# Expert 0 of a mixture-of-experts stage: gathering its rows in two halves with features on partitions

## The reference

```python
logits = (xt @ w_router + b_router)
top_vals, top_idx = lax.top_k(logits, TOP_K)
top_gates = jax.nn.softmax(top_vals, axis=-1)
...
def expert_block(args):
    xb, e = args
    gate = xb @ w_gate[e] + b_gate[e]
    up = xb @ w_up[e] + b_up[e]
    gate = jnp.minimum(gate, SWIGLU_LIMIT)
    up = jnp.clip(up, -SWIGLU_LIMIT, SWIGLU_LIMIT)
    glu = gate * jax.nn.sigmoid(SWIGLU_ALPHA * gate)
    return (glu * (up + 1.0)) @ w_down[e] + b_down[e]
```

## Time and profile before

| | |
|---|---|
| median of 3 runs | 1621.6 us (1621.21 to 1623.56) |
| span of the profiled execution | 1622.2 us |
| TensorE busy | 97% of the span |
| VectorE, ScalarE, GpSimd busy | 38%, 29%, 18% |
| transfers of phase B | 2,048 KB each |
| expert stage | from about 124.5 us to about 1036 us |

### The profile page before, as it was taken

One profiled execution on the slowest core, in us unless ns is written; L12 is line 12 of the kernel. 1 busy time (PEld: TensorE's weight loads), 2 busy tenths in 40 slices (PEclk: granted clock), 3 DMA queues, 4 the chain that ended last, 5 costly groups with the idle time before them and its releaser, 6 DMA issues. The chain is left out here.

```text
span 1622.2 us, 22330 instructions
## 1 busy us (share of the span) xinstructions
PE 1576.5 (97%) x9026; PEld 914.1 (56%) x9026; DVE 623.6 (38%) x1169; ACT 468.3 (29%) x703; POOL 286.7 (18%) x180
## 2 busy tenths in 40 slices
PE   9999999999999999999999999999999999999998
PEld 8843333333333333233233232598898899999986
DVE  7743212121212112121121121486586444478852
ACT  6421111111111111111111111466555554454443
POOL 3500000000000000000000000274234324445552
PEclk9999999999999999999999999999999999999999
DMA  9698999999999999999999999544324125555542
GB/s 350 216 379 339 427 427 426 426 429 426 427 427 428 427 426 427 427 428 428 428 428 428 427 428 428 216 153 156 105 105 156 58 99 208 179 168 187 182 182 104
DMA packets 93976, 507.66 MB, mean 313 GB/s; under 512 B 9020, under 2 KB 34665, under 8 KB 69321
## 3 DMA queue, kind: packets, MB, share of 16 engines
q1 hardware_dynamic: 93656, 505.97, 77.2%
q10 hardware_dynamic: 240, 0.55, 0.1%
HBM read 505.46 MB, written 1.05 MB: 312 GB/s over the span
## 5 line engine op out<-in xcount | busy, mean ns | idle before, releaser
L190 POOL TENSOR_TENSOR low<-ring,high 128x1024 fp32r<-128x1024 f32 x81 | 201.6, 2491 | 1275.6 <-ACT high L187 1275.5
L1684 PE MATMUL ps<-ring,x 128*64 128x512 f32 x1536 | 341.9, 595 | 21.4 <-DMA ring<-in_w_up 21.4
L1684 PEld LDWEIGHTS ps<-ring,x 128*64 128x64 f32 x1536 | 106.0, 137 | 253.2 <-issue 206.4
L187 ACT CAST high<-ring 128x1024 fp32r<-128x1024 f32 x162 | 167.8, 1049 | 192.7 <-PE ps L1850 115.7
L1846 PE MATMUL ps<-hTh,high 128*128 128x256 f32 x768 | 189.1, 284 | 0.5 <-PEq L2794 0.5
L1847 PE MATMUL ps<-hTl,high 128*128 128x256 f32 x768 | 188.4, 283 | 0.0
L1720 PE MATMUL ps<-ring,x 128*64 128x512 f32 x752 | 170.5, 595 | 0.0
L190 DVE TENSOR_TENSOR low<-ring,high 128x1024 fp32r<-128x1024 f32 x81 | 108.9, 1345 | 129.7 <-ACT high L187 129.6
L1846 PEld LDWEIGHTS ps<-hTh,high 128*128 128x128 f32 x768 | 147.3, 192 | 1.9 <-issue 1.5
L1847 PEld LDWEIGHTS ps<-hTl,high 128*128 128x128 f32 x768 | 147.4, 192 | 0.0
L1544 DVE TENSOR_SCALAR hT<-ps 128x512 f32<-128x512 f32 x32 | 22.1, 691 | 294.5 <-PE ps L1684 294.5
(11 more groups left out here) (503 smaller groups left out, 2105.3 us busy)
## 6 DMA issues: line engine op xcount, KB each, us to landing
ring<-in_w_down SPq DMA_DIRECT2D x52, 2048.0 KB, 32.8
ring<-in_w_gate SPq DMA_DIRECT2D x48, 2048.0 KB, 31.5
ring<-in_w_up SPq DMA_DIRECT2D x48, 2048.0 KB, 31.1
ring<-in_w_in SPq DMA_DIRECT2D x22, 2048.0 KB, 7.8
extra<-in_w_gate SPq DMA_DIRECT2D x16, 2048.0 KB, 32.0
extra<-in_w_up SPq DMA_DIRECT2D x16, 2048.0 KB, 29.8
extra<-in_w_down SPq DMA_DIRECT2D x14, 2048.0 KB, 34.7
ring<-in_w_up SPq DMA_DIRECT2D x22, 1024.0 KB, 7.2
```

Source lines behind the costliest of these rows:

```text
L187: eng.copy(hi, self.raw(u)).then_inc(self.sem("high_split"), 1)
L190: eng.tensor_tensor(lo, self.raw(u), hi.bitcast(F32), ALU.subtract).then_inc(self.sem(who + "_split"), 1)
L1684: last = pe.matmul(bank[h * CAP:(h + 1) * CAP, :], xg[:, c, kh, :], w[:, c, h * 512:(h + 1) * 512], start=False, stop=kh == 1 and c == 3)
```

## The change

The rows of expert 0 are no longer gathered with tokens on partitions. A new function `gather_columns` multiplies blocks of `xn` (128 tokens x 128 features) as weights with the picks (128 tokens x 64 places), so that the result has features on partitions at once. It does one half of the features, four blocks with two matmuls each (one for each half of the tokens). The first half is gathered at the end of phase A into bank 2 (the bank of G_), the second in phase B into bank 1 (ROWS), between the first and the second half of the gate product of expert 0. VectorE multiplies each half with its part of `g2` from its own bank. `rows_kept(0)` on ScalarE and `turned(0)` on TensorE are gone. The gate biases of expert 0 are added between the halves of its gate product, the up biases directly ahead of its up product; the first gate matmul now starts the bank (`start=True`). Experts 1 to 31 are as before.

```diff
-            pe.wait_ge(banks.free[ROWS_BANK], banks.uses[ROWS_BANK])
+            pe.wait_ge(banks.free[TURNED_BANK], banks.uses[TURNED_BANK])
             pe.wait_ge(sem("picks"), NT)
-            gather_rows(pe, banks.ps[:, ROWS_BANK, :], env["pick"], xn).then_inc(banks.full[ROWS_BANK], 1)
+            gather_columns(pe, banks.ps[:, TURNED_BANK, :], env["pick"], xn, 0).then_inc(banks.full[TURNED_BANK], 1)
...
+def gather_columns(pe, bank, pick, xn, h):
+
+    for c in range(4):
+        for t in range(NT):
+            last = pe.matmul(bank[:, c * CAP:(c + 1) * CAP], xn[:, t, h * 512 + c * P:h * 512 + (c + 1) * P], pick[:, t, :],
+                             start=t == 0, stop=t == NT - 1)
+    return last
...
-            v.tensor_scalar(hot[:, 0, :], ones[0:64, 0:CAP], fold[0:64, 0:1], None, ALU.mult).then_inc(sem("hot"), 1)
+            for h, use in enumerate((G_, ROWS)):
+                bank = bank_take(v, use, 0)
+                gains = env["g2"][:, 4 * h:4 * h + 4].unsqueeze(2).to_broadcast([P, 4, CAP])
+                bank_free(v.tensor_tensor(xg[:, :, h, :], bank[:, 0:4 * CAP].rearrange("p (c j) -> p c j", c=4), gains,
+                                          ALU.mult), use)
+                if h == 0:
+                    v.tensor_scalar(hot[:, 0, :], ones[0:64, 0:CAP], fold[0:64, 0:1], None, ALU.mult).then_inc(sem("hot"), 1)
...
-            gathered(0)
...
-            rows_kept(0)
...
-            turned(0)
             pe.wait_ge(sem("btab_in"), 48)
+
+            def second_columns():
+
+                bank_full(gather_columns(pe, bank_claim(pe, ROWS, 0), pick, xn, 1), ROWS)
...
+                whole = rnd is None and r == 0
+                both = [(0, GATE, bank_claim(pe, GATE, i)), (1, UP, None if whole else bank_claim(pe, UP, i))]
...
+                if not whole:
+                    pe.wait_ge(sem("hot"), i + 1)
+                    for m, use, bank in both:
+                        bias(m, bank)
                 bank_moved(pe, G_, i)
                 for m, use, bank in both:
                     for kh in range(2):
+                        if whole and m == 0 and kh == 1:
+                            second_columns()
+                            pe.wait_ge(sem("hot"), i + 1)
+                            bias(0, bank)
+                            bank_moved(pe, ROWS, i)
+                        if whole and m == 1 and kh == 0:
+                            bank = bank_claim(pe, UP, i)
+                            bias(1, bank)
```

More of the change, by code:

```diff
@@ L1366, in _ @@
             keep_busy(pe, banks.ps[:, banks.at["lgt"][0], :], ones, 2)
-            pe.wait_ge(banks.free[ROWS_BANK], banks.uses[ROWS_BANK])
+            pe.wait_ge(banks.free[TURNED_BANK], banks.uses[TURNED_BANK])
             pe.wait_ge(sem("picks"), NT)
-            gather_rows(pe, banks.ps[:, ROWS_BANK, :], env["pick"], xn).then_inc(banks.full[ROWS_BANK], 1)
-ROWS_BANK = 1
+            gather_columns(pe, banks.ps[:, TURNED_BANK, :], env["pick"], xn, 0).then_inc(banks.full[TURNED_BANK], 1)
+ROWS_BANK, TURNED_BANK = 1, 2
+def gather_columns(pe, bank, pick, xn, h):
[4 more added lines that the diff above has]
+    return last
 def gather_rows(pe, bank, pick, xn):
@@ L1671, in expert, with bias @@
                 nxt = i + 1 if rnd is None else pe.snap(i + 1)
-                pe.wait_ge(sem("hot"), i + 1)
-                both = [(0, GATE, bank_claim(pe, GATE, i)), (1, UP, bank_claim(pe, UP, i))]
-                for m, use, bank in both:
+                whole = rnd is None and r == 0
+                both = [(0, GATE, bank_claim(pe, GATE, i)), (1, UP, None if whole else bank_claim(pe, UP, i))]
+                def bias(m, bank):
                     for h in range(2):
                         pe.matmul(bank[h * CAP:(h + 1) * CAP, :], hot[32 * m:32 * m + 32, r % 2, :],
-                                  btab[32 * m:32 * m + 32, h * 512:(h + 1) * 512], start=True, stop=False)
+                                  btab[32 * m:32 * m + 32, h * 512:(h + 1) * 512], start=m == 1 or not whole, stop=False)
+                if not whole:
+                    pe.wait_ge(sem("hot"), i + 1)
+                    for m, use, bank in both:
+                        bias(m, bank)
                 bank_moved(pe, G_, i)
@@ L1684, in expert @@
                                 last = pe.matmul(bank[h * CAP:(h + 1) * CAP, :], xg[:, c, kh, :],
-                                                 w[:, c, h * 512:(h + 1) * 512], start=False,
+                                                 w[:, c, h * 512:(h + 1) * 512], start=whole and m == kh == c == 0,
                                                  stop=kh == 1 and c == 3)
```

## The result

| | median | range | span of the profiled execution |
|---|---|---|---|
| before | 1621.6 us (5 runs) | 1621.21 to 1623.56 | 1622.2 us |
| changed | 1626.18 us (5 runs) | 1623.96 to 1628.83 | 1624.4 us |

The ratio is 1.0027, 95% interval 1.0017 to 1.0038: the change made the kernel slower by 4.6 us. I had forecast 1622.1 us and no measurable change. The median lies above the range. The sum had the right sign, but with +0.5 us a ninth of the size.

What follows compares the result with a forecast made beforehand. The DMA stream of weight pieces bounds the expert stage. Piece 1 -1.6, piece 2 -0.5, piece 5 0 to +0.9; the latest wins, +0.5: span 1622.2 to 1622.7, less 0.6 gives 1622.1 us, range 1620.4 to 1623.6.

Steps and rivals of the forecast that it cites:

- The sum: Expert 0's changes added up: TensorE 1.5 us late from the up product on, +0.5 us at the end.
- the slack: How late expert 0's weight piece 5 may be issued without delaying the stream: 0.6 to 1.5 us.
- The frame: Expert stage: it ends when the last weight piece lands, so an edit counts by its effect on the stream.
- Part 1: Path to expert 0's first gate half product: it starts at 127.8 instead of 129.38, piece 1 issued 1.6 us earlier.
- The register read: Ahead of expert 0's first half product: TensorE reads the number of passes first, so the start was taken as 127.8.
- Part 2: Between the gate half products: gather 1.8 us, two biases 0.5, waiting 0.3; piece 2 issued at 137.5 instead of 136.5.
- Part 3: Behind the gate product: transposes, then up biases 0.5 us; up product at 138.2 instead of 136.72, TensorE 1.5 us late.
- second rival: VectorE's expert weights come late, the transposes wait, delay goes straight into piece 5: 1623.3 us, chance 0.10.
- The lower end: Piece 5's slack of 0.6 us, if a piece finding the queue empty needs 8.9 us, as piece 1 did.
- The upper end: Piece 5's slack of 1.5 us, reckoned by bytes: data wanted at 154.5, issue at 151.87, flow 1.1 us later.
- The first rival: The first piece decides; piece 5 has more slack than 1.5 us, stream keeps -0.5 to -1.6: 1620.0 to 1621.1, chance 0.26.
- The third: Rival: register read or instruction fetch holds TensorE until 129, first product not brought forward; 1623.3 us, chance 0.04.

Runs made afterwards that it cites:

- biasonly: Kernel before with only expert 0's biases moved: gate's between its product's halves, up's ahead of the up product; 1624.37 us, ratio 1.0015.
- delay1: Kernel before with two unused 256-column matmuls between expert 0's up product and the scatter, delaying piece 5 by 1.1 us; 1622.56 us, ratio 1.0003.
- both: Changed kernel with two unused matmuls in TensorE's idle time ahead of the first half product and the four biases in one row; 1623.92 us, ratio 1.0010.
- before_again: Kernel before, unchanged, run and profiled once more; 1621.55 us, ratio 0.9998.
- bias4: Changed kernel with expert 0's four gate and up biases in one row between the gate product's halves; 1625.40 us, ratio 1.0023.
- busy: Changed kernel with two unused 256-column matmuls filling TensorE's idle time ahead of the first gate half product; 1624.78 us, ratio 1.0018.
- early2: Changed kernel with the second gather in TensorE's idle time ahead of the first half product and four biases in one row; 1622.16 us, ratio 0.9999.
- delay2: Kernel before with four unused 256-column matmuls between expert 0's up product and the scatter, delaying piece 5 by 1.9 us; 1624.07 us, ratio 1.0014.

## Why the prediction was wrong, point by point

**The steps that failed.** The sum had TensorE 1.5 us late within expert 0, and of that 0.5 us reaching the end. TensorE was 4.3 us late. One term of 1.8 us was missing: the granted clock fell to 0.50 in the first half product, for which I had taken 3.5 us. One term was priced at half: the two pairs of biases, 1.0 us too little. And the lateness came through in full (4.6 us), because the stream has 0.1 to 0.8 us of slack and not 0.6 to 1.5. The sum missed by 4.1 us; about 2.8 of them are the first two, the rest is the slack.

**The frame held.** The stage ends with its last piece; TensorE's lateness in expert 0 reaches the end. No run contradicts it, and biasonly, a single edit, shows it with 2.6 us (1.0 to 3.9 by its interval); the 1.0 us of delay1 lie within its interval of nothing.

**Part 1 held but for one thing.** The first half product starts 3.41 us behind the gather's start, forecast 3.3. Eight short products take 1.97 us, forecast 1.8. The register read was the limit, as assumed: VectorE was done at 124.95, TensorE's read and what hangs on it ran from 124.6 to 125.3, and its first product began at 125.64. What the step lacked was the clock: the product ran 5.28 us instead of 3.5, **1.8 us that stood in no term**. I had read a clock of 1.00 in one profile of the kernel before and carried it over, though the change replaces products of 512 moving columns by products of 64 ahead of an idle time of the same length. The Trainium skill, "TensorE: Matmul & The Clock Gate" (HAM oscillation), describes a kernel with few rows whose clock falls again in each wait for a transfer. Its waits are longer than the 1.44 us here, so it doesn't foretell this fall, but it names the danger; a rival in which the clock falls was missing.

**Part 2 was mis-sized.** "Four took 1.02 us, two 0.5" is where: a pair takes 1.0, twice. The four lie in different parts of the array (two parts of the rows, two of the columns) and run side by side; a pair fills half of that room. The Trainium skill, "TensorE: Matmul & The Clock Gate" (Part 3, packing small matmuls), says that small matmuls at different row and column positions of the array run concurrently, and the trace agrees: 1.02 us for four, 1.00 for two. That is 1.0 us beyond the sum, less 0.3 of waiting for VectorE, which the longer biases now cover.

**Part 3 followed from these.** Forecast: the up product 1.5 us later. Measured: 4.3. The difference of 2.8 is 1.8 (clock) + 1.0 (biases) - 0.3 (wait) + 0.3 (both gathers and small handoffs). VectorE's expert weights ended at 136.88, TensorE asked at 137.44: no wait, as in the sum, so the second rival was not it.

**The slack was too large.** I gave piece 5 0.6 to 1.5 us; delay1 leaves 0.1 to 0.8 for a delay that begins there. The lower end rested on the 8.9 us of piece 1, but piece 5 took 8.7 to 11.1 us in the runs (9.5 in the earlier trace rows, 9.8 in the changed kernel). The upper end rested on bytes, as if the sixteen engines ran out together. It mattered at any size of the lateness: in both, with TensorE 1.7 us late, the time rose by 2.0 us, where my slack would have let 0.2 to 1.1 through. I also didn't reckon how late pieces 3 and 4 may be, and in the changed kernel they were 3.2 us late before piece 5 came into play.

**The first rival** (the first piece decides) falls: in both, piece 1 is issued 1.4 us early and the kernel is 2.0 us slower. What spoke for it fails too: where piece 2 follows 6.5 us behind piece 1, that one takes 8.0 to 8.9 us, and 7.8 to 9.1 where it follows after 3.4 to 4.6. The third falls too, since the product did come forward. The case that came wasn't on the list. And the range was too narrow for a kernel in which an unexpected 2 us anywhere in this stretch reaches the end at full price.

**Left open:** why the stream often settles later than piece 5's issue was late. Against before_again, the lateness of that issue and of the landings from piece 12 on are 4.3 and 4.6 us in the changed kernel, 3.3 and 3.6 in bias4, 2.7 and 3.8 in busy, 1.7 and 3.4 in both, 2.2 and 2.5 in biasonly, 0.5 and 1.0 in early2; only in delay1 the second is smaller (1.1 and 0.5). In busy, early2 and delay2 the landings lose another 1.2 to 1.5 us at piece 11, of which 0.8 to 1.1 stay; it was issued well before its turn. How the load lies on the sixteen DMA engines was not resolved, and whether it decides this isn't shown. Open too is by what exactly the clock falls: busy shows that it hangs on the idle time, delay2 that it can come behind the long products too, and no run keeps everything else and changes the length of the products alone. The biases' share of the time is known from the traces (1.0 us of TensorE) and not from the times, in which bias4 and both gain 0.8 and 0.9 us with intervals of 1.5 to each side.

## What to carry to other kernels

Where a stream of transfers sets the end, list for each of its next pieces when it is issued and how late it may be, and ask of an edit that brings the first one forward what it does to the second and the fifth; work that was hidden beside a wait and is moved between two releases costs its full time. Small matmuls that run side by side must be moved together. And when an edit puts short products and an idle time ahead of a long product, look for what keeps TensorE busy in between: two unused matmuls were worth 1.5 us here, and moving real work there, with the biases in one row (early2), was worth 4.

## What the runs showed of the hardware that I had not expected

- After eight products with 64 moving columns and 1.44 us of idle time the granted clock fell to 0.50 at about 126 us and was back at 1.00 before 130; one product took 5.35 instead of 3.65 us. In the kernels with the old gather the same place, four products with 512 moving columns and an idle time, is followed by 1.00 in five profiles and by 0.50 in one (delay2); the idle time is 1.33 to 1.36 us in all six.
- The fall also comes by accident elsewhere (0.50 from 40 to 42 us in the profiles of before, busy and biasonly). A fall at one place or the other came in 28 of 95 executions of the kernel before, and these took some 1.8 us longer than the rest: as much as many an edit to this kernel is worth.
- A matmul with 128x128 float32 weights takes 0.24 us with 64 moving columns, as with 32 and 129.
- Two bias products of 32 x 64 x 512 take 1.00 us, four in different parts of the array 1.02.
- A 2 MB piece issued into an empty queue lands 7.8 to 9.1 us after its issue (8.0 in the changed kernel, issued at 131.02), of which its bytes at 427 GB/s are 4.9. The Trainium skill, "DMA: Bandwidth & Descriptors" (the fit of cost per DMA, which it gives for transfers that GpSimd issues; these come from SyncE), would give an estimate of 6.8 us.
